# Second expert layer: from blocks of 128 slots in a loop to blocks of 32 slots over four column quarters, each expert's weights loaded once

## The reference

```python
hx = x * (1.0 + sc_f) + sh_f                    # shift and scale come from w_mod
gate = jnp.einsum('td,edf->tef', t, p['w_gate'])   # t: 512 x 1024, w_gate: 16 x 1024 x 256
up = jnp.einsum('td,edf->tef', t, p['w_up'])       # w_up: 16 x 1024 x 256
hid = jax.nn.silu(gate) * up * combine[..., None]  # combine: zero but for the token's two experts
return jnp.einsum('tef,efd->td', hid, p['w_down']) # w_down: 16 x 256 x 1024
x = layer_norm(alpha * x + g_f * hier_moe(hx), ln2_g, ln2_b)
```

## Time and profile before

| what | us |
|---|---|
| median of 3 runs | 3098.65 (3097.23 to 3103.58) |
| the profiled execution, its own time | 3100.13 |
| its span in the trace | 3098.4 |
| first expert layer: first gather to the end of the last block's stores | 707.9 to 1846.3 |
| second layer, choosing and places | 2795 to 2817 |
| second layer, blocks | 2817 to 3042 |
| combine, last layer norm, store of the output | 3042 to 3098 |

### The profile page before, as it was taken

The page is one execution under the profiler, slowest core; times in us unless marked ns, Lnnn a source line. Parts: engine busy times, 40 slices in busy tenths (PEclk is TensorE's granted clock), DMA queues, the critical chain, the costliest instruction groups (busy, mean ns, idle before and its releaser), DMA issues. The chain is left out here.

```text
span 3098.4 us, 44918 instructions
## 1 busy us (share of the span) xinstructions
PE 2356.9 (76%) x18284; PEld 1346.6 (43%) x18284; DVE 1055.1 (34%) x1828; ACT 752.6 (24%) x1810; POOL 128.9 (4%) x160
## 2 busy tenths in 40 slices
PE   5478737867999988888888954996697376766992
PEld 1177415653443433333333323886464246653440
DVE  0033545442222222222222216214665764442114
ACT  0031344521111101101010102214465413322331
POOL 0000000000000000000000001000000121000101
PEclk8789767987999998999999976998799587887996
DMA  9730300118899999999999954310000000315994
GB/s 377 316 104 4 119 20 1 62 57 326 350 363 397 406 406 403 396 402 402 401 397 404 401 234 160 108 43 18 1 1 1 1 1 8 116 42 200 363 362 152
DMA packets 182687, 644.73 MB, mean 208 GB/s; under 512 B 31880, under 2 KB 95240, under 8 KB 135392
## 3 DMA queue, kind: packets, MB, share of 16 engines
q1 hardware_dynamic: 160272, 596.26, 49.6%
q0 software_dynamic: 9360, 34.08, 3.0%
q10 hardware_dynamic: 12864, 11.67, 1.1%
HBM read 603.55 MB, written 38.42 MB: 207 GB/s over the span
## 5 line engine op out<-in xcount | busy, mean ns | idle before, releaser
L2002 PE MATMUL psum<-w,x 128*32 128x512 f32 x5696 | 674.2, 622 | 124.4 <-DMA w<-in_w_mlp 110.5
L2002 PEld LDWEIGHTS psum<-w,x 128*32 128x32 f32 x5696 | 182.5, 113 | 553.8 <-issue 403.1
L2153 DVE TENSOR_TENSOR u<-psum,x 128x512 f32<-128x512 f32 x89 | 61.6, 692 | 820.8 <-PE psum L2002 820.8
L2011 PE MATMUL psum<-w,act_turned 128*32 128x256 f32 x5696 | 329.6, 384 | 4.2 <-DVE act_turned L2162 3.6
L688 PE MATMUL psum<-high 128*128 128x512 f32 (+3 forms) x832 | 292.2, 351 | 36.9 <-DVE low L710 36.9
L688 PE MATMUL psum<-low,high 128*128 128x512 f32 (+3 forms) x832 | 291.0, 350 | 0.0
L688 PE MATMUL psum<-high,low 128*128 128x512 f32 (+3 forms) x832 | 291.0, 350 | 0.0
L2011 PEld LDWEIGHTS psum<-w,act_turned 128*32 128x32 f32 x5696 | 188.4, 112 | 174.4 <-issue 68.9
L710 DVE TENSOR_TENSOR low<-weight_slots,high 128x1024 fp32r<-128x1024 f32 (+3 forms) x84 | 89.3, 1066 | 290.2 <-ACT high L704 289.8
L688 PEld LDWEIGHTS psum<-high 128*128 128x128 f32 x832 | 159.5, 192 | 58.0 <-ACT high L704 37.8
L688 PEld LDWEIGHTS psum<-high,low 128*128 128x128 f32 x832 | 159.5, 192 | 20.1
(11 more groups left out here) (488 smaller groups left out, 2841.7 us busy)
## 6 DMA issues: line engine op xcount, KB each, us to landing
w<-in_w_mlp SPq DMA_DIRECT2D x192, 2048.0 KB, 29.3
weight_slots<-in_w_ada SPq DMA_DIRECT2D x12, 2048.0 KB, 12.3
weight_slots<-in_w_mod SPq DMA_DIRECT2D x12, 2048.0 KB, 12.6
weight_slots<-in_w_in SPq DMA_DIRECT2D x9, 2048.0 KB, 8.2
weight_slots<-in_w_gate SPq DMA_DIRECT2D x36, 512.0 KB, 6.4
weight_slots<-in_w_up SPq DMA_DIRECT2D x36, 512.0 KB, 8.9
down<-in_w_down SPq DMA_DIRECT2D x18, 1024.0 KB, 10.4
weight_slots<-in_w_out SPq DMA_DIRECT2D x6, 2048.0 KB, 10.3
```

The costliest lines, as they stand in the source:

```text
L2002: mm = pe.matmul(psum[g * RB:(g + 1) * RB, bank, :], b.turned[:, kc, q * RB:(q + 1) * RB], w[:, i, g * BANK:(g + 1) * BANK], start=kc == 0 ...
L2011: mm = pe.matmul(psum[g * RB:(g + 1) * RB, 2 + parity, 0:YW], b.act_turned[:, parity, kc, :], w[:, i, g * YW:(g + 1) * YW], start=kc == 0, ...
L2153: step.reach(dve.tensor_tensor(b.u[:], psum[:, bank, :], b.bias[:, parity], ALU.add), s.biased, at + 1)
```

## The change

It gives the second layer the form that the first has. `BY_RANK2` sets 40 blocks of 32 slots for the 15 largest experts (6, 6, 4, 3, 3, eight times 2, 1, 1); the sixteenth gets none and goes to the extra blocks. Experts are taken from both ends of the ranking in turn, so the 15 turns have 6, 1, 6, 1, 4, 2, 3, 2, 3, 2, 2, 2, 2, 2 and 2 blocks. The blocks are written out; four share one gather of 128 rows, so there are 10 tiles of rows. Six experts' weights fit at once (`HELD`); a turn from the seventh on waits until the last block of the turn six before has used that place. Each of the three matrices comes in one DMA of 1 MB, with neighbouring rows on one partition, so that a run is 8 KB in all three. The first product of a block is 32 matmuls of 128 columns (64 of gate and 64 of up), the second 8 of 256. `places` and its helpers go; `places_by_rank` serves both layers. Shift and scale are read from DRAM in the order of the new layout, so `modulations` stores two more parts of the second layer's vectors as rows (four stores more), the stage loads them and DVE adds 1 to the scale. ACT's queue stores the results.

```diff
+BY_RANK2 = [6, 6, 4, 3, 3] + [2] * 8 + [1, 1, 0]
+OVER2 = L * 2 // RB + 4
...
-             if (cp * span + c * BANK) // D in (2, 5)]
+             if (cp * span + c * BANK) // D in layers[work[g][0]].as_rows]
...
+    Q = P // RB
+    FW, YW = FF2 // Q, D // Q
+    HELD = 6
...
+        def load_gu(engine, e, slot, landed):
+            for a, w in enumerate((args.w_gate_2, args.w_up_2)):
+                engine.dma_start(b.gu[:, slot, a].rearrange("p (k n) -> p k n", k=DC),
+                                 w[0][ds(e, 1)].rearrange("a (p k) n -> p (a k) n", k=DC)).then_inc(landed, 16)
+
+        def load_down(engine, e, slot, landed):
+            engine.dma_start(b.down[:, slot].rearrange("p (k n) -> p k n", k=fk),
+                             args.w_down_2[0][ds(e, 1)].rearrange("a (p k) n -> p (a k) n", k=fk)).then_inc(landed, 16)
...
+            for turn in range(turns):
+                e = sync.value_load(r.order[0:1, ranks[turn]:ranks[turn] + 1], min_val=0, max_val=E2 - 1)
+                if turn >= HELD:
+
+                    sync.wait_ge(s.used, done["first", last_of[turn - HELD]])
+                load_gu(sync, e, turn % HELD, gu_landed[turn % HELD])
+                if turn >= HELD:
+
+                    sync.wait_ge(s.used, done["second", last_of[turn - HELD]])
+                load_down(sync, e, turn % HELD, down_landed[turn % HELD])
...
+            for t in range(tiles):
+                if t >= 2:
+
+                    pool.wait_ge(s.x_turned, t - 1)
+                    pool.wait_ge(gathered[t % 2], 16 * (t // 2))
+                pool.indirect_dma_start(b.rows[:, t % 2], None, rows,
+                                        bass.IndirectOffsetOnAxis(ap=r.slot_token[:, t:t + 1], axis=0))\
+                    .then_inc(gathered[t % 2], 16)
...
+            def first_product(slot, half, q, bank):
+                for m in range(DC):
+                    for g in range(Q):
+                        mm = pe.matmul(psum[g * RB:(g + 1) * RB, bank, 0:2 * FW].rearrange("p (a n) -> p a n", a=2),
+                                       b.turned[:, half, m, q * RB:(q + 1) * RB],
+                                       b.gu[:, slot, :, m * FF2 + g * FW:m * FF2 + (g + 1) * FW],
+                                       start=m == 0, stop=m == DC - 1)
+                return mm
+
+            def second_product(slot, parity):
+                for m in range(fk):
+                    for g in range(Q):
+                        mm = pe.matmul(psum[g * RB:(g + 1) * RB, 2 + parity, 0:YW], b.act_turned[:, parity, m, :],
+                                       b.down[:, slot, m * D + g * YW:m * D + (g + 1) * YW],
+                                       start=m == 0, stop=m == fk - 1)
+                return mm
...
+            for what, at in order:
+                turn, _ = blocks[at]
+                t = at // Q
+                if what == "first":
+                    if at % Q == 0:
+                        pe.wait_ge(s.x_kept, t + 1)
+                    if at >= 2:
+
+                        pe.wait_ge(s.activated, at - 1)
+                    pe.wait_ge(gu_landed[turn % HELD], 32 * (turn // HELD + 1))
+                    first_product(turn % HELD, t % 2, at % Q, at % 2).then_inc(s.used, 1)
+                else:
+                    pe.wait_ge(s.act_ready, at + 1)
+                    if at >= 2:
+
+                        pe.wait_ge(s.y_kept, at - 1)
+                    pe.wait_ge(down_landed[turn % HELD], 16 * (turn // HELD + 1))
+                    second_product(turn % HELD, at % 2).then_inc(s.used, 1)
+                free(what, at)
+                if what == "second" and at % Q == Q - 1 and t + 2 < tiles:
+                    turn_tile(t + 2)
...
+            act.dma_start(b.mods[:], k.rows2[0:1, 3 * D:5 * D].rearrange("o (a p k) -> (o p) a k", a=2, k=DC))\
+                .then_inc(s.mods_loaded, 16)
+            act.wait_ge(s.scaled, 1)
+            keep_rows(0)
+            keep_rows(1)
+            silu(0)
+            for at in range(n):
+                if at + 1 < n:
+                    silu(at + 1)
+                keep_y(at)
+                if at % Q == Q - 1 and at // Q + 2 < tiles:
+                    keep_rows(at // Q + 2)
...
+            for at in range(n):
+                if at:
+
+                    dve.wait_ge(s.act_ready, at)
+                activate(at, at % 2)
+                if at >= 2:
+
+                    dve.wait_ge(s.used, done["second", at - 2])
+                turn_act(at % 2)
...
-                places(core, k, "places2", r, b.oneh, b.mask, experts, top, n_blocks, True)
+            places_by_rank(core, k, f"places{which}", r, b.oneh, b.mask, args.layout1 if first else args.layout2, experts, top,
+                           static_tiles * P, over, tiles)
```

More of the change, by code:

```diff
@@ L2260, in _ @@
         def _(pool):
-            last = last_block(pool, r, n_blocks // 2, n_blocks)
-            def gather(j, q):
-                gather_tokens(pool, s, b.slot_ids[:, q:q + 1], b.rows[:, q], r, rows, j, gathered[q])
-            gather(0, 0)
-            gather(1, 1)
-            with pool.Fori(0, last) as i:
-                for q in range(2):
-                    j = i * 2 + q
-                    pool.wait_ge(s.x_turned, j + 2)
-                    pool.wait_ge(gathered[q], i * 16 + 16)
-                    pool.sem_inc(s.taken, 1)
-                    gather(j + 2, q)
@@ L2276, in _ @@
-            for q in range(2):
-                pool.wait_ge(gathered[q], last * 16 + 16)
+            for t in range(tiles):
[5 more added lines that the diff above has]
+                    .then_inc(gathered[t % 2], 16)
@@ L2369, in _, with silu @@
-            keep_rows(1, 1)
-            silu(0, 0)
-            with act.Fori(0, last) as i:
-                for q in range(2):
-                    j = i * 2 + q
-                    keep_rows(j + 2, q)
-                    silu(j + 1, 1 - q)
-                    keep_y(j)
-            silu(last * 2 + 1, 1)
-            keep_y(last * 2)
-            keep_y(last * 2 + 1)
+            def silu(at):
+                act.wait_ge(s.used, done["first", at])
+                if at >= 2:
+                    act.wait_ge(s.activated, at - 1)
+                act.activation(b.sil[:, at % 2], psum[:, at % 2, 0:FW], ACT.Silu).then_inc(s.silued, 1)
@@ new lines, in keep_y @@
+            def keep_y(at):
+                t, q = at // Q, at % Q
+                act.wait_ge(s.used, done["second", at])
+                if q == 0 and t >= 2:
+                    act.wait_ge(y_stored[t % 2], 16 * Q * (t // 2))
+                act.copy(b.y[:, t % 2, q], psum[:, 2 + at % 2, 0:YW]).then_inc(s.y_kept, 1)
+                if q == Q - 1:
+                    act.wait_ge(s.y_kept, at + 1)
+                    for g in range(Q):
+                        act.dma_start(y_rows[t * P:(t + 1) * P, g * YW:(g + 1) * YW].rearrange("(q r) n -> r q n", r=RB),
+                                      b.y[g * RB:(g + 1) * RB, t % 2]).then_inc(y_stored[t % 2], 16)
@@ L2381, in _ @@
+            act.wait_ge(s.y1_stored, 16 * Q * (tiles // 2))
+            act.wait_ge(s.y0_stored, more * (16 * Q) + 16 * Q * (tiles // 2))
+            act.sem_inc(s.taken, 1)
         @block.vector
         def _(dve):
[L2383 to L2388 removed]
```

398 lines of the change are left out of this document (133 added, 265 removed).

## The result

The changed kernel takes 3066.9 us (median; 3066.3 to 3067.3), the kernel before 3101.1 on the same chip: ratio 0.9895, 95% interval 0.9882 to 0.9908. By the ratio that is about 33 us faster (29 to 37); the forecast was 50.6. The profiled executions say where the time went. The span fell by 33.9 us: -38.6 in the second layer's stage from the table of slots to combine (225.3 to 186.8), +3.5 in places (13.5 to 17.0), +1.8 ahead of the end of choosing, -0.6 after combine starts.

What follows compares the result with a forecast made beforehand. TensorE, busy throughout the second layer's blocks, was taken as the bound, with DMA close behind (share 0.97). Stage -55.3, places +4.2 and modulations +0.5 sum to -50.6 us: from 3098.65 to 3048 us, range 3034 to 3082.

Steps and rivals of the forecast that it cites:

- the prediction's own case: Whole kernel: the forecast's terms hold, DMA ends last in the second layer's stage; 3034 to 3062 us, chance 0.74.
- rival A: Second layer's first products: load and stream one after the other, 3.4 us each, TensorE bounds; 3062 to 3096 us, chance 0.17.
- TensorE's pace: Second layer's blocks: 0.118 us a round of four quarters, first product 1.9, block 2.83, 40 blocks 113 us.
- TensorE's path, 145 us: Second layer's stage: start 11.7, blocks 113, transposes 8, ACT's tiles 12; TensorE through at 145 us, never waiting for weights.
- the 12 us for ACT's tiles: After each fourth block, ACT's stores and tile write-out delay the next silu: 1.3 us a tile, 9 times.
- DMA, not TensorE, ends last: Second layer's stage: the fifteenth expert's weights land at 151.5 us after the table, against TensorE's 145.
- Rival B: Second layer's blocks: TensorE's instruction packets arrive late, 10.4 us each, some 26; slower, kernel 3170 us, chance 0.06.
- Extra block: End of the stage: weights and stores until 160.9 us, then serial 2.3, 1.5, 0.95 and 4.3; stage 170 us.
- Start: Second layer's stage: first product starts 11.7 us after the table of slots.
- Places: From the end of choosing to the table of slots: 17.7 us instead of 13.5, +4.2 (bounds 2 and 9.6).
- Modulations: Four more stores, two of them at the end at 0.25 us each: +0.5 us.
- Rival C: Second layer's stage: more extra blocks than one, 17 us each, three more giving 3099 us; chance 0.03.

Runs made afterwards that it cites:

- e3: Changed kernel with only the first six experts' weights (and the extra block's) loaded, later blocks reusing them; 3045.9 us, ratio 0.9831 to the kernel before.
- e8: Changed kernel with every second contraction chunk of each first product left out, all weights still fetched; 3040.7 us, ratio 0.9817 to the kernel before.
- e4: Changed kernel without the loop over extra blocks, so ten pairs of token and expert are not computed; 3049.4 us, ratio 0.9846 to the kernel before.
- e7: Changed kernel with the extra block written out as forty-first block of the list, loops left out; 3054.6 us, ratio 0.9861 to the kernel before.
- e6: Changed kernel with no weights issued until the first gather of 128 rows has landed; 3061.9 us, ratio 0.9884 to the kernel before.
- e2: Changed kernel with gate and up in runs of 1 KB, down 4 KB, old row order; 3068.3 us, ratio 0.9901 to the kernel before.
- e1: Changed kernel with each weight matrix in two DMAs, runs of 4 KB instead of 8; 3062.7 us, ratio 0.9883 to the kernel before.

## Why the prediction was right and wrong

The direction held, and so did the range, but for a reason that was not forecast. The gain was 17 us too large, and what was to set the end, the transfers, did not. 3066.9 lies outside the range of the prediction's own case (3034 to 3062) and inside the one given to rival A, whose mechanism did not occur; the stated range took in half of A, and that it covers the result is luck. By its own steps:

- **TensorE's pace** (rounds of 0.118 us, first product 1.9, block 2.83): right, and a little better. The product takes 1.93, the block 2.61 us. Rival A, the rule of the Trainium skill, TensorE: Matmul & The Clock Gate, "What overlaps and what doesn't", falls: it would need 3.4 us, while here 64 loads and 64 matmul instructions with all rows in use fit into 1.93.
- **TensorE's path, 145 us**: it was 169.5 (last listed product at 2991.8). Faster blocks gave back up to 40 x 0.22 = 9 (at the undisturbed pace), and of the 12 us for ACT's tiles TensorE waited 2.4. Against that stand the start, 15.9 instead of 11.7, the gaps, 22, and the granted clock:

```profile
2853.26:2856.67 3.41, 3.41 (x60) 3.06 (x51) 0.47 (x2) 0.24 (x2) 0.00 (x0) 0.50 1.03 420
2897.64:2901.05 3.41, 3.41 (x69) 3.31 (x65) 0.32 (x2) 0.37 (x1) 0.00 (x0) 0.50 1.04 425
```

  Together with the first 1.4 us of the blocks these are 8.2 us at 1.2 GHz instead of 2.4, in which half the work gets done, so 4 us are lost. The first products are busy for more than that, about 13 us over 40 x 1.93 (93.9, less 3.6 of the extra block's). A product that a gap cuts in two counts some 0.3 us more than a whole one (1.69 + 0.53 at 2880.38), which makes some 5 of it; the remaining 4 are not resolved. With the queues empty from 2881 on (e3) the path is 149.5, with 6.7 us of gaps in it. So 145 was near for a TensorE that is hardly kept from its instructions, but as a sum: its start was 4 too low, its blocks up to 9 and its tiles 10 too high, and it had nothing for the clock and for small pauses between products.
- **"DMA, not TensorE, ends last"**: this is the step that failed. The margin was 6.5 us of 151.5, that is 0.16 us a block (rival A's "from about 2.5 us on" should read 2.1 with the prediction's own 145). 151.5 us for the weights was itself a little long: 140.2 for the last gate and up in e8, and in the changed kernel q1 moved 50.33 MB in 0.657 x 186.8 us, 410 GB/s instead of 399. TensorE's path was 169.5 instead of 145, with 22 us of it in a term that the forecast had at nothing, the wait for instructions.
- **Rival B** named the cause of the failure: instructions that don't arrive, with nobody as releaser. It was priced at 10.4 us a packet and so as a slower kernel, deciding from 7.7. The packets come every 6.4 us. The prediction made a case of its own out of it (chance 0.06), all or nothing, and the forecast's sum has no term for it. Between 4.2 us (what TensorE uses) and 7.7 lies a loss that does not turn the sign: 26 packets x 6.4 = 166 us for the blocks, from the first product on, already above the 151.5 of the DMA path. The evidence against it, "256 in 7.2 us with no gap", came from products at a pace of 7.2 us a packet or slower, where a packet every 6.4 us is in time; it could not speak for 4.2. The Trainium skill, Runtime: NRT & Kernel Launch, "Instruction fetch mechanics", calls a page's fetch mostly hidden. Here that holds with idle DMA engines (e3) and not with full ones.
- **Extra block**: forecast to wait for its weights until 160.9 and take 9.1 after them. It waited for no weights. The serial steps took 17.3 us from the last listed product:

```profile
2991.84 1.13 PE L2161 MATMUL psum<-ident,rows 128*128 128x128 f32 x8
...
2992.24 1.80 ACTq L2267 DMA_DIRECT2D slot_rows<-y  x4
2995.28 2.26 ACT L2290 ACTIVATE turned<-psum,mods,scale 128x32 f32 x8 [3.07 <-issue]
2997.97 3.64 PE L2174 MATMUL psum<-gu,turned 128*32 128x128 f32 x64 [5.00 <-ACT turned L2290]
3002.84 1.94 PE L2183 MATMUL psum<-down,act_turned 128*32 128x256 f32 x16 [1.23 <-DVE act_turned L2321]
...
3005.64 1.81 ACTq L2306 DMA_DIRECT2D slot_rows<-y  x4
3009.09 0.33 SPq L2370 DMA_DIRECT2D gate<-rows  x1
```

  ScalarE issues the last tile's stores (1.8 us), then sits idle for 3.07 us without a releaser, where the loop is entered, writes out the rows (2.26), and after TensorE's 5 us of idleness the granted clock is 0.50 and both products run at half pace (3.64 against 1.93, 1.94 against 1.05). The forecast had none of the first three, and 2.3 and 0.95 for the products. Its sum from the listed blocks to combine came out about right (15, measured 17.3) by luck: a wait for weights that did not happen stood in for them. e4 prices the block at 13.0, e7 gets 6.0 back.
- **Start**: 11.7 us, for which the prediction shows no working; measured 15.9. The first gather, issued together with the weights, took 9.0 us; in the kernel before, issued 0.4 us ahead of them, 6.3; alone (e6) 4.3. e6 shows that the gather is not all of it: the weights then come later, and the stage stays at 186.7.
- **Places** +4.2 forecast, +3.5 measured. **Modulations** +0.5: no loss seen; they end 1.35 us earlier. The 1.8 us ahead of the end of choosing are within the spread of that point from run to run.
- **Rival C**: one extra block, as forecast.

Open: why a packet comes only every 6.4 us beside full queues, whatever their depth and packet size. Its own transfer takes 1.1 us of that and TensorE resumes 1.2 to 1.6 us after it; the rest is not told apart. The runs show that it is so, and that it ends with the transfers. A layout that takes fewer instructions for the same columns under full queues was not tried.

## What to carry to other kernels

Count the instructions an engine uses up per microsecond next to the rate at which they can come: written-out TensorE code of short matmuls (160 instructions in 2.6 us) starved here beside full data queues, and idle time without a releaser, at equal counts of instructions, is how it looked. A rival priced as all or nothing also has a middle, and its middle belongs in the forecast's sum. A remainder that is worked off serially in a loop can cost several times its share of the work (13.0 us here for a block of 2.6); in the written-out list it shares the drain of the last block.

## What was not expected of the hardware

Besides the 6.4 us a packet: a gather of 128 rows lands in a median of 7.7, 8.8 and 9.9 us beside weights in runs of 1, 4 and 8 KB (e2, e1, changed kernel), and the first one in 4.3 with nothing beside it (e6). The instruction packets do not follow that: they come every 6.3 to 6.5 us (median) in all three. Four column quarters at 128 columns go at 0.12 us a round of four matmul instructions, loads included. And of the seven gaps of over 2 us in the changed kernel two (ended at 2852.23 and 2896.64) were followed 1 us later by a granted clock of 0.50 for 3.4 us, which adds about 1.7 us to the gap's own price; the other five were not.
